# Layer order behind the routed experts: the last expert part in four loads, transposes by halves, chunk rests ahead of additions, the last two feed-forward parts by quarters

## The reference

```python
x = x + merged @ w_out                                  # two attentions, gated
x = x + routed_experts(rmsnorm(x, g_ffn), ...)          # top 4 of 32, d_expert 1024
hp = rmsnorm(x, g_ple)
x = x + sigmoid(hp @ w_ple_gate) * (p_i @ w_ple_proj)
x = x + 0.5 * swiglu(rmsnorm_2(x, ffn1_norm), ffn1_w_gu, ffn1_w_down)     # d_ff 2816
h = rmsnorm_2(x, mix_norm)                              # two mixers, one w_in, one w_out
x = x + mixed @ w_out
x = x + memory_cross_attention(rmsnorm_2(x, mem_q_norm), ...)
x = x + 0.5 * swiglu(rmsnorm_2(x, ffn2_norm), ffn2_w_gu, ffn2_w_down)
return rmsnorm_2(x, final_norm)

def swiglu(h, w_gu, w_down):
    gate, up = split(h @ w_gu, 2)
    return (silu(gate) * up) @ w_down
```

## Time and profile before

| | us |
|---|---|
| median of 3 runs | 1798.98 (1796.70 to 1799.46) |
| the profiled execution, its time | 1796.77 |
| its span on the core | 1795.0 |
| TensorE busy | 1659.9 (92%), granted clock 0.986 on average |
| VectorE busy | 681.1 (38%) |
| ScalarE busy | 551.4 (31%) |
| bytes read | 544 MB, 304 GB/s over the span |

### The profile page before, as it was taken

One profiled execution on the slowest core, in us unless ns is written; L12 is line 12 of the kernel. 1 busy time (PEld: TensorE's weight loads), 2 busy tenths in 40 slices (PEclk: granted clock), 3 DMA queues, 4 the chain that ended last, 5 costly groups with the idle time before them and its releaser, 6 DMA issues.

```text
span 1795.0 us, 21429 instructions
## 1 busy us (share of the span) xinstructions
PE 1659.9 (92%) x9479; PEld 1072.4 (60%) x9480; DVE 681.1 (38%) x826; ACT 551.4 (31%) x748; POOL 24.4 (1%) x37
## 2 busy tenths in 40 slices
PE   8999899798889999998878888989999999999998
PEld 7788433333334454442323233379997998989996
DVE  5897411112121211211111111176554865566543
ACT  6576200011111111100000011174443765454341
POOL 1000000000000000000000000000000000000000
PEclk9999999999999999999999999999999999999999
DMA  7537799999999999999999999945555423445552
GB/s 254 169 129 258 281 418 428 427 426 428 428 422 405 411 423 409 423 421 427 427 429 428 427 425 426 413 159 189 180 187 192 146 95 134 160 139 174 182 189 93
DMA packets 125871, 546.48 MB, mean 304 GB/s; under 512 B 5632, under 2 KB 73344, under 8 KB 101104
## 3 DMA queue, kind: packets, MB, share of 16 engines
q1 hardware_dynamic: 124448, 540.96, 76.2%
q0 software_dynamic: 1040, 4.00, 0.7%
q10 hardware_dynamic: 288, 0.11, 0.0%
HBM read 544.00 MB, written 1.05 MB: 304 GB/s over the span
## 4 chain that ended last, share of the span: by engine, by line
PE 56%; DMA 21%; DVE 2%; ACT 1%; issue 1%; DVEq 0%
DMA ring<-in_w_down 21%; PE PS L859 9%; PE PS L821 7%; PE PS L1006 6%; PE PS L521 6%; PE PS L522 6%; PE PS L523 6%; PE PS L870 2%; PE PS L778 1%; PE PS L488 1%; PE PS L490 1%; PE PS L489 1%; PE PS L803 1%; PE PS L1046 1%; PE PS L957 1%
## 5 line engine op out<-in xcount | busy, mean ns | idle before, releaser
L821 PE MATMUL PS<-ring,work 128*64 128x512 f32 x2048 | 454.0, 595 | 34.1 <-DMA ring<-in_w_gate_up 34.1
L1821 DVE TENSOR_TENSOR ring<-ring,ring 128x2048 fp32r<-128x2048 f32 (+2 forms) x130 | 289.4, 2234 | 305.2 <-ACT ring L1245 305.1
L821 PEld LDWEIGHTS PS<-ring,work 128*64 128x64 f32 x2048 | 142.1, 137 | 326.6 <-issue 251.5
L1245 ACT CAST ring<-ring 128x2048 fp32r<-128x2048 f32 (+2 forms) x131 | 242.5, 1861 | 210.5 <-DMA ring<-in_mem_w_kv 89.1
L859 PE MATMUL PS<-ring,work 128*64 128x512 f32 x1024 | 247.0, 628 | 56.9 <-DMA ring<-in_w_down 43.5
L859 PEld LDWEIGHTS PS<-ring,work 128*64 128x64 f32 x1024 | 78.2, 143 | 212.0 <-issue 174.0
L2234 DVE TENSOR_SCALAR work<-PS 128x512 f32<-128x512 f32 x32 | 22.1, 690 | 333.3 <-PE PS L821 333.3
L521 PE MATMUL PS<-xr,ring 128*128 128x256 f32 x480 | 136.6, 285 | 1.1 <-DVE xr L2304 1.1
L522 PE MATMUL PS<-xr,ring 128*128 128x256 f32 x480 | 135.8, 283 | 0.0
L523 PE MATMUL PS<-xr,ring 128*128 128x256 f32 x480 | 135.8, 283 | 0.0
L1502 ACT ACTIVATE work<-work 128x512 f32<-128x512 f32 x32 | 20.1, 630 | 374.1 <-DVE work L2234 374.1
(11 more groups left out here) (404 smaller groups left out, 2225.8 us busy)
## 6 DMA issues: line engine op xcount, KB each, us to landing
ring<-in_w_gate_up SPq DMA_DIRECT2D x128, 2048.0 KB, 17.5
ring<-in_w_down SPq DMA_DIRECT2D x64, 2048.0 KB, 16.2
ring<-in_ffn_w_gu SPq DMA_DIRECT2D x44, 1024.0 KB, 5.2
ring<-in_w_in SPq DMA_DIRECT2D x28, 1024.0 KB, 5.4
ring<-in_ffn_w_down SPq DMA_DIRECT2D x22, 1024.0 KB, 4.8
ring<-in_w_out SPq DMA_DIRECT2D x8, 1024.0 KB, 5.2
ring<-in_mem_w_kv SPq DMA_DIRECT2D x8, 1024.0 KB, 14.1
ring<-in_w_ple_gate SPq DMA_DIRECT2D x4, 1024.0 KB, 12.0
```

What stands on the lines that cost most here:

```text
L821: t = e.matmul(PS[hf * 64:hf * 64 + 64, bank, :], XG[g % 2][:, 2 * kp + kk, i * 64:(i + 1) * 64], chunks(raw(w), w)[:, kk, c0 + hf * 512:c ...
L1245: e.copy(hi(j), raw(j)).then_inc(*act.now(("hi", j)))
L1821: e.tensor_tensor(lo(j), raw(j), hi(j).bitcast(F32), ALU.subtract).then_inc(*dve.now(("lo", j)))
```

## The change

Four kinds of edits, all from the last expert to the end:

- The second down part of expert 31 (`tail`) is loaded by four DMAs of 512 KB, one for each of its four k rows, with a semaphore each, and TensorE waits for each before the two products that use it.
- Behind the experts TensorE transposes x by halves of columns: as soon as quarter (h, nb) is added, its four chunks.
- VectorE's order at the entries: at "ple" the last addition goes ahead of a split, at "mix" and "ffn2" both chunk pairs are turned ahead of the last addition, and the split behind it (at "mix" behind the factor), at "mem" both are turned ahead of the last addition. In `renormed` the rest of a chunk pair follows right behind the scaling of the next pair.
- The last two parts of both down projections run by quarters.

```diff
--- before.py
+++ after.py
@@ -312,6 +312,8 @@
         o_dma, o_pe, o_v, o_a = [sem("o_dma0"), sem("o_dma1")], sem("o_pe"), sem("o_v"), sem("o_a")
         o_go = {n: sem(f"o_go_{n}") for n in ("pe", "dve", "act")}
         o_bias = sem("o_bias")
+        tail = of["down", NE - 1][1]
+        tail_in = [sem(f"tail{k}_loaded") for k in range(3)]
 
 
         x = x_t[:, :].rearrange("p (h n) -> p h n", h=2)
@@ -853,8 +855,11 @@
                     if kp:
                         beside(n + 1)
                     w = of["down", n][kp]
-                    e.wait_ge(*ready(w))
+                    if w != tail:
+                        e.wait_ge(*ready(w))
                     for kk in range(4):
+                        if w == tail:
+                            e.wait_ge(*((tail_in[kk], 16) if kk < 3 else ready(w)))
                         for dh in range(2):
                             t = e.matmul(PS[dh * 64:dh * 64 + 64, BDN, :], HT[:, kk, kp * 64:kp * 64 + 64],
                                          chunks(raw(w), w)[:, kk, dh * 512:(dh + 1) * 512], start=kp == 0 and kk == 0,
@@ -971,10 +976,14 @@
 
 
             pe.stage("ple")
-            for i in range(4):
+            for nb in range(2):
                 for h in range(2):
-                    e.wait_ge(*dve["x_after", h, i // 2])
-                turn_pair(x, 2 * i, 2, 4 + i, ("ple_t", i))
+                    e.wait_ge(*dve["x_after", h, nb])
+                    for c in range(4 * nb, 4 * nb + 4):
+                        t = e.transpose(PS[:, 4 + c // 2, (c % 2) * 256 + h * 128:(c % 2) * 256 + h * 128 + 128],
+                                        x[:, h, c * 128:(c + 1) * 128], ident)
+                        if h and c % 2:
+                            t.then_inc(*pe.now(("ple_t", c // 2)))
             for part in range(2):
                 for h in range(2):
                     tok_part(xT, of["ple_gate", 0], part, h, PS[:, h, :], ("ple", 0, h),
@@ -995,7 +1004,7 @@
                     if blk > 1:
                         e.wait_ge(*dve[f, "hT", blk - 2])
                     feat(xT, of[f, "up", blk][0], bg + 1, (f, "up", blk))
-                for kp in range(10):
+                for kp in range(9):
                     w = of[f, "down", kp][0]
                     e.wait_ge(*ready(w))
                     e.wait_ge(*dve[f, "hT", kp])
@@ -1010,16 +1019,19 @@
 
             def ffn_last(f, h, nb, end=False):
 
-                w = of[f, "down", 10][0]
                 hs = slice(h * 128, (h + 1) * 128)
-                if h + nb == 0:
-                    e.wait_ge(*ready(w))
-                    e.wait_ge(*dve[f, "hT", 10])
-                for kk in range(2):
-                    for z, half in ((0, hi(w)), (0, lo(w)), (1, hi(w))):
-                        t = e.matmul(PS[:, 4 + 2 * h + nb, :], hT[z][:, 20 + kk, hs],
-                                     chunks(half, w)[:, kk, nb * 512:(nb + 1) * 512], start=False, stop=kk == 1 and z == 1,
-                                     skip_group_check=True)
+                for kp in (9, 10):
+                    w = of[f, "down", kp][0]
+                    if h + nb == 0:
+                        e.wait_ge(*ready(w))
+                        e.wait_ge(*dve[f, "hT", kp])
+                    for kk in range(2):
+                        for z, half in ((0, hi(w)), (0, lo(w)), (1, hi(w))):
+                            t = e.matmul(PS[:, 4 + 2 * h + nb, :], hT[z][:, 2 * kp + kk, hs],
+                                         chunks(half, w)[:, kk, nb * 512:(nb + 1) * 512], start=False,
+                                         stop=kp == 10 and kk == 1 and z == 1, skip_group_check=True)
+                    if end and kp == 9:
+                        t.then_inc(*pe.now(("w", w)))
                 t.then_inc(*pe.now((f, "down", h, nb), *([("w", w)] if end else [])))
 
             def ffn_two(f):
@@ -2293,16 +2305,20 @@
             def renormed(name, base, gain_name, dst, key):
 
                 e.wait_ge(*act["RS", name])
+                def what_is_left(i):
+                    e.wait_ge(*act["xN", name, i])
+                    e.tensor_tensor(dst[1][:, 2 * i:2 * i + 2, :], PS[:, base + i, :].rearrange("p (c t) -> p c t", c=2),
+                                    dst[0][:, 2 * i:2 * i + 2, :].bitcast(F32), ALU.subtract).then_inc(*dve.now((key, i)))
+
                 for i in range(4):
                     for c in range(2):
                         ps = PS[:, base + i, c * 256:(c + 1) * 256]
                         t = e.scalar_tensor_tensor(out=ps, in0=ps, scalar=gain(gain_name, 2 * i + c), in1=RS, op0=ALU.mult,
                                                    op1=ALU.mult)
                     t.then_inc(*dve.now(("xn", name, i)))
-                for i in range(4):
-                    e.wait_ge(*act["xN", name, i])
-                    e.tensor_tensor(dst[1][:, 2 * i:2 * i + 2, :], PS[:, base + i, :].rearrange("p (c t) -> p c t", c=2),
-                                    dst[0][:, 2 * i:2 * i + 2, :].bitcast(F32), ALU.subtract).then_inc(*dve.now((key, i)))
+                    if i:
+                        what_is_left(i - 1)
+                what_is_left(3)
 
             first = of["ffn1", "gate", 0][0]
             ple_out(0, 0)
@@ -2312,8 +2328,8 @@
             ple_out(1, 0)
             for i in range(2):
                 turned(xT2, i, 4 + i, "ffn1_norm_2", "ffn1T")
+            ple_out(1, 1)
             lo_to(first + 1)
-            ple_out(1, 1)
             factor("ple")
             for i in (2, 3):
                 turned(xT2, i, 4 + i, "ffn1_norm_2", "ffn1T")
@@ -2368,11 +2384,11 @@
             ffn("ffn1")
             for nb, h in ((0, 0), (0, 1), (1, 0)):
                 ffn_out("ffn1", "mix", h, nb)
-            turned(mix_xT, 0, 0, "mix_norm_2", "mixT")
+            for i in range(2):
+                turned(mix_xT, i, i, "mix_norm_2", "mixT")
+            ffn_out("ffn1", "mix", 1, 1)
+            factor("mix")
             lo_to(of["qf", 0][0])
-            ffn_out("ffn1", "mix", 1, 1)
-            turned(mix_xT, 1, 1, "mix_norm_2", "mixT")
-            factor("mix")
             for i in (2, 3):
                 turned(mix_xT, i, i, "mix_norm_2", "mixT")
             renormed("mix", 0, "mix_norm_2", xT, "mixN")
@@ -2512,9 +2528,9 @@
             lo_to(of["mem_q", 1][0])
             for nb, h in ((0, 0), (0, 1), (1, 0)):
                 residual("mem", h, nb, 4 + 2 * nb + h, ("out2", nb, h))
-            turned(oT, 0, 0, "mem_q_norm_2", "mem_qT")
+            for i in range(2):
+                turned(oT, i, i, "mem_q_norm_2", "mem_qT")
             residual("mem", 1, 1, 7, ("out2", 1, 1))
-            turned(oT, 1, 1, "mem_q_norm_2", "mem_qT")
             factor("mem")
             for i in (2, 3):
                 turned(oT, i, i, "mem_q_norm_2", "mem_qT")
@@ -2569,10 +2585,10 @@
                 residual("ffn2", h, 0, h, ("mem_o", 0, h))
             lo_to(of["mem_o", 1][1] + 1)
             residual("ffn2", 0, 1, 2, ("mem_o", 1, 0))
-            turned(xT, 0, 4, "ffn2_norm_2", "ffn2T")
+            for i in range(2):
+                turned(xT, i, 4 + i, "ffn2_norm_2", "ffn2T")
+            residual("ffn2", 1, 1, 3, ("mem_o", 1, 1))
             lo_to(of["mem_o", 1][1] + 2)
-            residual("ffn2", 1, 1, 3, ("mem_o", 1, 1))
-            turned(xT, 1, 5, "ffn2_norm_2", "ffn2T")
             factor("ffn2")
             for i in (2, 3):
                 turned(xT, i, 4 + i, "ffn2_norm_2", "ffn2T")
@@ -2659,7 +2675,12 @@
                         src = rows(w, p.k0, p.k, p.c0, p.n)
                     else:
                         src = w[p.expert][p.k0 * 128:(p.k0 + p.k) * 128, :].rearrange("(p k) n -> p k n", p=128)
-                    e.dma_start(chunks(raw(j), j), src).then_inc(loaded[plan.slot[j]], 16)
+                    if j == tail:
+                        for k in range(3):
+                            e.dma_start(chunks(raw(j), j)[:, k, :], src[:, k, :]).then_inc(tail_in[k], 16)
+                        e.dma_start(chunks(raw(j), j)[:, 3, :], src[:, 3, :]).then_inc(loaded[plan.slot[j]], 16)
+                    else:
+                        e.dma_start(chunks(raw(j), j), src).then_inc(loaded[plan.slot[j]], 16)
 
 
             load_to(of["down", CHECK - 2][1] + NS)
```

## The result

The changed kernel took 1789.91 us (median of 5 runs, 1788.55 to 1790.28) against 1798.14 us (5 runs, 1796.70 to 1799.46) of the kernel before, side by side on one chip: a ratio of 0.9949 (0.9939 to 0.9960), faster by 8.2 us. The forecast was 1792, with 1789.5 to 1796.2 as its range. So the direction and the places were right, and the time fell near the range's low edge: the sum of 6.1 us was too small.

The account below looks back on a forecast made before the run. Weight DMA was taken to set the pace in the experts, TensorE behind them, idling for VectorE. Gains 0.28 + 0.8 + 2.46 + 0.42 + 0.73 + 1.42 = 6.1 us, taken from 1797.9, gave 1792; range 1789.5 to 1796.2.

Parts of the forecast that it names:

- Turning by halves: Behind the experts, transposing x by halves completes chunk pair 0 after two more transposes instead of four: 0.28 us gained.
- First block: First feed-forward block: an earlier factor and interleaved scalings and rests gain 0.8 us; a wait moves to the split.
- the wait for pair 2: First feed-forward block: TensorE asks for chunk pair 2 at 1211.6, gets it at 1211.9, waiting 0.3 us.
- at most 0.3 us of wait: Sign of being right: TensorE enters the two feed-forward stages with no more wait than this.
- Into the mixers: Entry into the mixers: turning both chunk pairs ahead of the addition closes TensorE's whole gap, 2.46 us gained.
- first rival: Through the mixers, moved splits make VectorE late and gaps return; 3.2 us of gain left, 1794.7 us; chance 0.14.
- Memory attention and second block: Same reordering closes gaps at 1535.82 and 1599.38, and interleaving the one at 1611.61: 0.42 + 0.73 us gained.
- The end: Last down projection by quarters: the last addition of x starts right behind TensorE's last product, 1.42 us gained.
- The moved load: One mixers load starts some 5 us later but lands 1.4 us before ScalarE's cast: cost 0.
- Four loads: Last expert part: TensorE reaches it 2.1 us after landing and queued loads pay nothing extra; 0 booked.
- second rival: At the last expert, slow loads delay ScalarE's cast and row copy; at 8.7 us, 1800.4 us, slower; chance 0.04.

Follow-up runs that it names:

- e1: Changed kernel with the last expert part in one load again: 1790.55 us, ratio 0.9955.
- e2: Changed kernel with parts 0 to 9 of both down projections over all quarters again: 1791.36 us, ratio 0.9964.
- e5: Kernel before with only the interleaving of scalings and rests in `renormed` put in: 1798.13 us, ratio 0.9997.
- e6: Kernel before with only both turnings ahead of the last addition at the memory attention put in: 1796.65 us, ratio 0.9990.
- e8: As e7, plus the last combination taking high halves first and the final scaling and output in column halves: 1787.30 us, ratio 0.9941.
- e7: Changed kernel with cast and split of the first feed-forward block's first up part ahead of the third gate quarter: 1790.43 us, ratio 0.9949.
- e3: Changed kernel with VectorE's old order at the entry into the mixers, quarters kept: 1792.27 us, ratio 0.9960.
- e4: Changed kernel with both the quarters and the order at the mixers undone: 1796.03 us, ratio 0.9989.

## Why the prediction was right, and where it was wrong

**Turning by halves, 0.28.** Measured 0.28 (4.76 to 4.48). The shape was not as told: the transposes start sooner (idle 0.30 instead of 1.00), and most of that is given back before the gate product (0.51 instead of 0.30) and in transposes that now wait in their midst (2.45 us instead of 2.26). That the number came out to the hundredth is luck.

**First block, 0.8.** Measured 0.82. The wait did move to the split: 0.99 us behind L1833 where 1.12 stood. The scaling starts 34.12 us behind the gate's first product instead of 34.67 (forecast 0.46 earlier, measured 0.55), and the wait for pair 2 is 0.24 (forecast 0.3). One of the prediction's own signs was not met, "at most 0.3 us of wait" into this stage, since its text had already moved a wait of this size to the split. The idle times were mispriced here too, but on both sides: the first full product now starts 9.17 us behind the second half product instead of 10.37, 1.20 earlier for a gap of 1.07, and the new gap of 0.24 costs 0.50 (the starts on either side of it are 0.52 and 0.22 us apart instead of 0.12). The errors nearly cancelled.

**Into the mixers, 2.46.** Measured 2.72. The first rival (the gaps return further on) fell: the views name no gap behind it.

**Memory attention and second block, 0.42 + 0.73.** Measured 0.65 + 0.95.

**The end, 1.42.** Measured 1.39, with the last addition 0.04 us behind TensorE's end (forecast: within 0.1). The moved load cost nothing: ScalarE casts its last part there at 1389.73, right behind its own work and with no wait for a DMA.

**The step that failed is the price of a gap.** The sum took three places, the mixers, the memory attention and the second block, at their printed idle times of 2.46, 0.42 and 0.73 us; they gave 2.72, 0.65 and 0.95. Such a time starts at the modelled end of the last product and leaves out the slow start of the next; each closed place gave back 0.22 to 0.26 us more, 0.71 in all, which turns 6.1 into 6.8.

**And a term was missing.** In the profiled execution the clock stayed up behind the gap, and no row of it could show that in other executions it falls. The forecast put this at nothing. Half of the six that hold the gap lost another 1.5 us (1.48 to 1.54), which is some 0.76 on average. With it the traces give 6.82 + 0.76 = 7.6 us. The means of the runs of the two kernels in this study, 1798.4 (the 55 that other kernels were compared with) and 1790.6 (12), differ by 7.8 (6.8 to 8.7, 95%). The first comparison's 8.2 and the second one's 7.2 lie on either side. That the share is a half is an estimate from six executions.

**Four loads.** 0 booked, 0 measured. The mechanism of the second rival, ScalarE's cast of the first gate part standing ahead of its copy of the last expert's rows, does exist, but with loads of either kind. In e1, e2, e5 and e6 the cast came so late that TensorE waited 1.93 to 2.14 us for the last combination instead of 1.41; three of these four have one load, one has four. ScalarE in e1:

```profile
1167.34 1.90 ACT L1254 CAST ring<-ring 128x2048 fp32r<-128x2048 f32 x1 [6.98 <-DMA ring<-in_w_ple_gate]
1169.14 0.58 ACT L1455 CAST work<-PS 128x512 fp32r<-128x512 f32 x1
```

That nothing is won holds for executions in which the part lands in time. In e5, with one load, it landed at 1162.1 (1143.8 + 18.3), and TensorE stood still for it:

```profile
1162.15 3.65 PE L859 MATMUL PS<-ring,work 128*64 128x512 f32 x16 [1.27 <-DMA ring<-in_w_down]
```

None of the eight traces with four loads has such a wait, and one of the six with one load has it. Even there the wait set nothing further on: ScalarE's cast ran from 1164.65 to 1166.55 and its copy of the rows came right behind it, 0.7 us after TensorE was done. And over all traces the four loads brought the last combination no earlier: it stands at 1168.7 us on average with one load (six traces) and at 1169.4 with four (seven, without e8, whose combination is another).

**What stays open.** What moves the last combination by 6 us between executions wasn't tried. Medians of 5 runs can't tell a difference under 2 us for that reason, and e7's gain of 2.0 us in the trace is not seen in its median. Whether it is the gap that brings the low clock, and in what share of executions, rests on three cases.

## What to carry to other kernels

Before an engine that runs its program in order, put the instruction that the bottleneck waits for ahead of whatever nobody waits for yet: moving one 2.28 us split and one addition gave back 2.7 us. Price a gap of TensorE from start to start, not from the printed idle time, and allow for a low clock behind a gap like the one of 2.46 us here. And where two edits close the same gap (the order 2.72, the quarters 1.36), book it once, and take them back singly and together to see which one carries it.

## What the runs showed of the hardware

- A gap of 2.46 us was followed in three of six executions by TensorE's lower clock (1.2 GHz), beginning at the gap's end or up to 1.3 us behind it and costing 1.5 us each time; in the other three, and in the eight without this gap, the clock stayed at its upper level (2.4 GHz) there. One profile can't tell such a cost.
- Four loads of 512 KB in one queue landed their last byte 5.0 us behind the part ahead, just as one load of 2 MB did. The Trainium skill, DMA: Bandwidth & Descriptors, section "Anatomy of one DMA", puts some 2 us of fixed cost on each DMA that GpSimd issues. The loads here are issued by SyncE, and with more loads waiting in the queue none of that cost was seen between their landings.
- Kernels that are the same up to the last combination (the changed one, e2, e3, e4 and e7) reached it anywhere between 1166.2 and 1172.2 us, while the 620 us behind it repeated within 0.1 us in four traces (the changed kernel three times, and e1).
